# HGRN level products in blocks of 64 tokens, and another order for the end of the HGRN stage

## The reference, cut to what matters

```python
def step(s, inp):                       # one chunk, for HGRN
    qc, kc, vc, gc = inp
    g = jnp.cumsum(gc, axis=1)          # gc: log of the forget gate, per token and key channel
    o_inter = einsum('bthk,bhkv->bthv', qc * exp(g), s)
    diff = where(mask, g[:, :, None] - g[:, None, :], -inf)
    att = einsum('bthk,bshk,btshk->bhts', qc, kc, exp(diff))
    o_intra = einsum('bhts,bshv->bthv', att, vc)
    s_new = exp(g_last)[..., None] * s + einsum('bshk,bshv->bhkv', kc * exp(g_last - g), vc)
```

## Time and profile before

| | us |
|---|---|
| median of 3 runs | 1561.28 |
| lowest, highest | 1557.97, 1569.07 |
| the profiled execution | 1559.14 |
| its span, first to last instruction | 1557.1 |
| stage_hgrn in it | 534.9 to 575.1 |

### The profile page before, as it was taken

How to read it: one execution, slowest core, us unless ns; L and a number is a source line. 1 busy time by engine, 2 the same in 40 slices (tenths; PEclk the granted TensorE clock), 3 DMA queues, 4 the chain that set the end, 5 groups by cost and what they waited for, 6 DMA issues and landing times.

```text
span 1557.1 us, 37799 instructions
## 1 busy us (share of the span) xinstructions
PE 1522.2 (98%) x17035; PEld 971.1 (62%) x17035; DVE 527.0 (34%) x782; ACT 369.8 (24%) x560; POOL 44.9 (3%) x51
## 2 busy tenths in 40 slices
PE   9989999999999889999999999999999999999997
PEld 8976799999999866943533533534435435335344
DVE  6468656553569668451101111011011011010113
ACT  4248444442437467220000000000000000000001
POOL 0000000000000000000000000000000000000000
PEclk9999999999999999999999999999999999999999
DMA  9566645543445462699999999999999999999996
GB/s 356 202 230 211 198 128 167 184 162 143 136 167 176 154 159 64 239 367 420 369 388 418 417 410 417 410 417 415 411 416 418 411 417 417 412 417 415 412 413 234
DMA packets 144490, 479.48 MB, mean 308 GB/s; under 512 B 32184, under 2 KB 61632, under 8 KB 129747
## 3 DMA queue, kind: packets, MB, share of 16 engines
q1 hardware_dynamic: 141404, 469.07, 78.0%
q0 software_dynamic: 2064, 5.66, 0.9%
q10 hardware_dynamic: 871, 2.42, 0.4%
HBM read 463.55 MB, written 13.55 MB: 306 GB/s over the span
## 4 chain that ended last, share of the span: by engine, by line
PE 57%; DVE 0%; ACT 0%; DVEq 0%; issue 0%
PE ps L3146 37%; PE ps L3162 19%; PE ps L3122 0%; PE ps L3208 0%; PE ps L3190 0%; PE ps L3171 0%; PE ps L3196 0%; PE ps L3178 0%; DVE act L3367 0%; DVE act L3357 0%; DVE tail_rows L3357 0%; DVEq L3013 0%; ACT xn_tokens L3423 0%; DVE at_first L3244 0%; PE ps L3129 0%; ACT item_y L3408 0%
## 5 line engine op out<-in xcount | busy, mean ns | idle before, releaser
L3146 PE MATMUL ps<-up_ring,item_x 128*32 128x448 f32 x6000 | 565.6, 539 | 0.0
L3146 PEld LDWEIGHTS ps<-up_ring,item_x 128*32 128x32 f32 x6000 | 195.0, 110 | 365.5 <-issue 364.3
L3162 PE MATMUL ps<-down_ring,hid_t 128*32 128x256 f32 x5376 | 291.5, 379 | 0.0
L3162 PEld LDWEIGHTS ps<-down_ring,hid_t 128*32 128x32 f32 x5376 | 175.0, 110 | 117.6 <-issue 3.9
L3329 DVE TENSOR_TENSOR hid<-hid,ps 128x1344 f32<-128x1344 f32 x16 | 24.9, 1555 | 650.4 <-PE ps L3146 649.0
L476 DVE TENSOR_TENSOR w_lo_dense<-ring,w_hi_dense 128x2048 fp32r<-128x2048 f32 x53 | 121.3, 2291 | 99.5 <-ACT w_hi_dense L470 99.4
L470 ACT CAST w_hi_dense<-ring 128x2048 fp32r<-128x2048 f32 x53 | 100.9, 1903 | 89.4 <-PE ps L493 82.0
L3408 ACT COPY item_y<-ps 128x512 f32<-128x512 f32 x8 | 4.7, 586 | 422.2 <-PE ps L3162 422.2
L1684 PE MATMUL ps<-x_hi_dense,w_hi_dense 128*128 128x288 f32 x352 | 95.1, 296 | 1.8 <-PEq L1571 1.8
L1685 PE MATMUL ps<-x_lo_dense,w_hi_dense 128*128 128x288 f32 x352 | 94.9, 297 | 0.0
L3404 ACT ACTIVATE hid<-ps 128x1344 f32<-128x1344 f32 x16 | 20.6, 1290 | 265.6 <-PE ps L3146 243.2
(11 more groups left out here) (522 smaller groups left out, 1699.7 us busy)
## 6 DMA issues: line engine op xcount, KB each, us to landing
up_ring<-in_we_dram SPq DMA_DIRECT2D x250, 896.0 KB, 8.7
down_ring<-in_we_dram SPq DMA_DIRECT2D x112, 1024.0 KB, 11.2
ring<-in_w_ffn_dram SPq DMA_DIRECT2D x23, 1024.0 KB, 7.9
ring<-in_w_in_odd_dram SPq DMA_DIRECT2D x9, 2048.0 KB, 7.8
ring<-in_w_in_even_dram SPq DMA_DIRECT2D x5, 2048.0 KB, 16.3
ring<-in_w_ffn_dram SPq DMA_DIRECT2D x5, 2048.0 KB, 7.5
ring<-in_w_out_odd_dram SPq DMA_DIRECT2D x3, 2048.0 KB, 8.1
odd_layer<-in_we_dram SPq DMA_DIRECT2D x6, 896.0 KB, 12.2
```

The source lines that it names most:

```text
L3146: mm = pe.matmul(k.ps[32 * q:32 * q + 32, 3 * w + g, 0:FW], xg[:, c, g, :], block_of[:, q, :], start=c == 0, stop=c == DC - 1, skip_group_ ...
L3162: mm = pe.matmul(k.ps[32 * q:32 * q + 32, 6 + g // 2, 256 * (g % 2):256 * (g % 2) + 256], hidT[:, 2 * r + j, g, :], block_of[:, j, 256 * q ...
```

## The change

1. The diagonal and levels 0 to 4 are computed in blocks of 64x64 tokens: 16 products (32 pairs) where there were 32 (64 pairs). A gather is 512 columns wide where it was 256; the masks for it are made for blocks of 64.
2. The sample tokens get a place of their own: PSUM banks 7, 3 and 4 for the diagonal and levels 0 and 1, an own tile `att_samples`, own masks, and three small VectorE instructions of 32 columns.
3. ScalarE's copies into `att`: six (four of 32x32 for the samples, two of 64x512) where there were four, and ahead of level 5's copy, which now has to come after them. The constants' tables and `att_blocks` keep the same room in total.
4. The end: `state_samples` 0 to 3 stand together ahead of dot(7), in four banks (6, 7, 4, 2), so that `new_state` 0 to 3 follow one another; 4 and 5 come where 2 and 3 were, 6 and 7 where 4 and 5 were, ahead of the prompt's final state. `scale_state` comes earlier on ScalarE, and so do two copies of the convolution's last rows (`turn_last`, `take_last`).

```diff
@@ -106,14 +106,16 @@
-    s, q = p[:, None] % 32, np.arange(32)[None, :]
-    c["block_diagonal"] = (s == q) * 1.0
-    lv = []
-    for l in range(5):
-        h = 1 << l
-        lv.append((s // (2 * h) == q // (2 * h)) & (s % (2 * h) < h) & (q % (2 * h) >= h))
-    c["level"] = np.stack(lv, 1).reshape(P, -1)
-    c["room_for_gains"] = np.zeros((P, 672))
+    def block_masks(block, levels):
+        s, q = p[:, None] % block, np.arange(block)[None, :]
+        masks = [s == q]
+        for h in (1 << l for l in range(levels)):
+            masks.append((s // (2 * h) == q // (2 * h)) & (s % (2 * h) < h) & (q % (2 * h) >= h))
+        return np.stack(masks, 1).reshape(P, -1) * 1.0
+
+    c["level"] = block_masks(64, 5)
+    c["level_samples"] = block_masks(TS, 2)
+    c["room_for_gains"] = np.zeros((P, 384))
@@ -2043,7 +2045,8 @@
-        att32 = k.sb(s, "att_blocks", [P, 9, 32])
+        att64 = k.sb(s, "att_blocks", [P, 8, 64])
+        att_s = k.sb(s, "att_samples", [P, TS])
@@ -2082,14 +2085,15 @@
-        blocks_of = lambda bank: k.ps[:, bank, 0:9 * 32].rearrange("p (n j) -> p n j", j=32)
+        blocks_of = lambda bank: k.ps[:, bank, :].rearrange("p (n j) -> p n j", j=64)
...
+        samples_bank = lambda l: 3 + l
...
-        SIDE, SUM = (6, 7), (3, 5, 4)
+        SIDE, SUM = (6, 7, 4, 2, 6, 7, 6, 7), (3, 5, 4)
@@ -2150,23 +2154,24 @@
-                    mask = k.const("level")[:, 32 * l:32 * l + 32].bitcast(I32)
-                    n = 9 if l <= 1 else 8
-                    then(dve.copy_predicated(att32[:, 0:n, :], mask.unsqueeze(1).broadcast_to([P, n, 32]), blocks_of(bank_of(l))[:, 0:n, :]),
-                         n_["level_in"])
+                    mask = k.const("level")[:, 64 * l + 64:64 * l + 128].bitcast(I32)
+                    if l <= 1:
+                        dve.copy_predicated(att_s[:, :], k.const("level_samples")[:, TS * l + TS:TS * l + 2 * TS].bitcast(I32),
+                                            k.ps[:, samples_bank(l), 0:TS]).then_inc(*dve_step.up())
+                    then(dve.copy_predicated(att64[:, :, :], mask.unsqueeze(1).broadcast_to([P, 8, 64]), blocks_of(bank_of(l))), n_["level_in"])
...
-                    dve.wait_ge(*n_["state_dot"].at(i + 1 + (i >= 6)))
+                    dve.wait_ge(*n_["state_dot"].at(i + 1))
...
-                        dve.tensor_tensor(at, at, k.ps[:, SIDE[i % 2], :].rearrange("p (b v) -> p b v", b=4), ALU.add).then_inc(*n_["state_new"].up())
+                        dve.tensor_tensor(at, at, k.ps[:, SIDE[i], :].rearrange("p (b v) -> p b v", b=4), ALU.add).then_inc(*n_["state_new"].up())
...
-                                                       k.ps[:, SIDE[i % 2], P * (b % 4):P * (b % 4) + P], ALU.mult, ALU.add)
+                                                       k.ps[:, SIDE[i], P * (b % 4):P * (b % 4) + P], ALU.mult, ALU.add)
@@ -2179,8 +2184,10 @@
-                then(dve.tensor_tensor(att32[:, :, :], blocks_of(5), k.const("block_diagonal").unsqueeze(1).broadcast_to([P, 9, 32]), ALU.mult),
+                dve.tensor_tensor(att_s[:, :], k.ps[:, 7, 0:TS], k.const("level_samples")[:, 0:TS], ALU.mult).then_inc(*dve_step.up())
+                then(dve.tensor_tensor(att64[:, :, :], blocks_of(5), k.const("level")[:, 0:64].unsqueeze(1).broadcast_to([P, 8, 64]), ALU.mult),
...
+                dve.wait_ge(*dve_step.all())
@@ -2195,14 +2202,14 @@
                 new_state(3)
-                leave(0)
                 new_state(4)
                 new_state(5)
+                leave(0)
+                new_state(6)
                 leave(1)
...
                 dve.tensor_tensor(out[:, :, TP:T], by_head(k.ps[:, 2, 0:P]), rss, ALU.mult).then_inc(*n_["out"].up())
-                new_state(6)
                 new_state(7)
@@ -2264,27 +2271,30 @@
                 act.copy(kds[:, :], k.ps[:, 6, 0:P]).then_inc(*n_["kd_copied"].up())
+                take_last(1)
+                take_last(2)
+                act.wait_ge(*n_["zeroed"].at(2))
+                act.wait_ge(*n_["level_in"].at(6))
+                for a in range(0, P, TS):
+                    act.copy(att[a:a + TS, 8, a:a + TS], att_s[a:a + TS, :]).then_inc(*n_["blocks_in"].up())
+                for a in range(0, P, 64):
+                    act.copy(att[a:a + 64, 0:8, a:a + 64], att64[a:a + 64, :, :]).then_inc(*n_["blocks_in"].up())
+                act.wait_ge(*n_["blocks_in"].at(6))
                 act.wait_ge(*n_["inter_dot"].at(1))
                 act.copy(from_state[:, :], k.ps[:, 7, 0:P]).then_inc(*n_["inter_taken"].up())
-                act.wait_ge(*n_["zeroed"].at(2))
                 take_blocks(5)
-                take_last(1)
-                act.wait_ge(*n_["level_in"].at(6))
-                for a in range(0, P, 32):
-                    ins = act.copy(att[a:a + 32, :, a:a + 32], att32[a:a + 32, :, :])
-                ins.then_inc(*n_["blocks_in"].up())
+                scale_state(4)
                 take_blocks(6)
-                scale_state(4)
+                scale_state(5)
                 act.wait_ge(*dotted(7, 1))
                 act.copy(attx[:, :, :], k.ps[:, 3, :].rearrange("p (c n) -> p c n", c=4)).then_inc(*attx_in.up())
-                take_last(2)
                 act.wait_ge(*dt_turned.at(1))
...
                 square(0)
-                scale_state(5)
+                scale_state(6)
                 square(1)
@@ -2292,9 +2302,8 @@
-                scale_state(6)
...
-                act.wait_ge(*n_["state_dot"].at(7))
+                act.wait_ge(*n_["state_dot"].at(9))
@@ -2304,16 +2313,16 @@
-                        mm = pe.matmul(k.ps[TS * c:TS * c + TS, bank, 8 * 32:9 * 32], x1[:, c, TP:T], x2[:, c, TP:T], start=True, stop=True,
+                        mm = pe.matmul(k.ps[TS * c:TS * c + TS, bank, 0:TS], x1[:, c, TP:T], x2[:, c, TP:T], start=True, stop=True,
...
-                            for a in range(0, P, 32):
-                                at, n = slice(P * i + a, P * i + a + 32), 4 * i + c
-                                mm = pe.matmul(k.ps[a:a + 32, bank, 32 * n:32 * n + 32], x1[:, c, at], x2[:, c, at], start=True, stop=True,
+                            for a in range(0, P, 64):
+                                at, n = slice(P * i + a, P * i + a + 64), 4 * i + c
+                                mm = pe.matmul(k.ps[a:a + 64, bank, 64 * n:64 * n + 64], x1[:, c, at], x2[:, c, at], start=True, stop=True,
@@ -2334,17 +2343,19 @@
+                    if l == 5:
+                        pe.wait_ge(*n_["level_in"].at(3))
...
-                        pe.wait_ge(*n_["blocks_in"].at(1))
+                        pe.wait_ge(*n_["blocks_in"].at(7))
...
-                                mm = samples_dot(bank, x1, x2)
+                                mm = samples_dot(samples_bank(l), x1, x2)
@@ -2364,10 +2375,13 @@
                         pe.wait_ge(*n_["inter_taken"].at(1))
-                    if i >= 2:
-                        pe.wait_ge(*n_["state_new"].at(i - 1))
+                        pe.wait_ge(*last_copied.at(3))
+                    if i == 2:
+                        pe.wait_ge(*n_["blocks_in"].at(7))
+                    if i >= 4:
+                        pe.wait_ge(*n_["state_new"].at(i - 3 if i < 6 else i - 1))
                     r = slice(TS * c, TS * c + TS)
-                    pe.matmul(k.ps[:, SIDE[i % 2], :], kds[r, :], vbd[r, 4 * hf:4 * hf + 4, :], start=True, stop=True).then_inc(*n_["state_dot"].up())
+                    pe.matmul(k.ps[:, SIDE[i], :], kds[r, :], vbd[r, 4 * hf:4 * hf + 4, :], start=True, stop=True).then_inc(*n_["state_dot"].up())
 
@@ -2375,9 +2389,10 @@
-                samples_dot(5, k0, q).then_inc(*n_["diag_dot"].up())
+                samples_dot(7, k0, q).then_inc(*n_["diag_dot"].up())
...
+                pe.wait_ge(*n_["level_in"].at(1))
@@ -2387,7 +2402,10 @@
+                turn_last(1)
...
+                pe.wait_ge(*last_copied.at(1))
+                turn_last(2)
@@ -2396,14 +2414,10 @@
                 dot(5)
-                turn_last(1)
                 dot(6)
-                state_samples(0)
-                state_samples(1)
-                pe.wait_ge(*last_copied.at(1))
-                turn_last(2)
+                for i in range(4):
+                    state_samples(i)
                 dot(7)
-                pe.wait_ge(*last_copied.at(2))
                 for m, src in enumerate((dta["acum"], dt, dta["wend"])):
@@ -2427,32 +2441,30 @@
 
-                pe.wait_ge(*n_["blocks_in"].at(3))
+                pe.wait_ge(*n_["blocks_in"].at(8))
                 pe.wait_ge(*attx_in.at(1))
...
                 y_prompt(1)
-                state_samples(2)
-                state_samples(3)
+                state_samples(4)
+                state_samples(5)
                 pe.wait_ge(*dt_copied.at(5))
...
                 sum_squares(0)
-                pe.wait_ge(*last_copied.at(3))
+                pe.wait_ge(*n_["state_new"].at(4))
```

(8 more changed lines are left out.)

## The result

The changed kernel takes 1553.88 us (median of 20 runs, 1549.77 to 1564.95) against 1561.32 us (20 runs, 1557.33 to 1569.86). The ratio is 0.9958, 95% interval 0.9946 to 0.9971: 4.5 to 8.4 us faster, 6.6 by the ratio. The forecast was 4.6 us faster, 1556.0 us, in a range of 1551.5 to 1562.0. The profiled execution shows the stage from 535.95 to 568.65.

A forecast was written before the change was run, and what follows sets the result against it. A chain across engines with TensorE instruction halts bounds stage_hgrn, and a us saved there is one of the program; 4.4 - 0.9 + 1.1 = 4.6 us gives 1554.5 or 1556.7, 1556.0 us taken, range 1551.5 to 1562.0.

The forecast's parts named there:

- main term: Level products: with no halts for instruction pieces, dot(5) is done 4.4 us sooner.
- Matmul 175: End of an instruction piece in the stage, now in dot(3): needed at about 542.7, delivered by 542.3, no halt.
- The rival by which the halts stay: Level products: halts belong to the DMA load, not the count; vector work makes it 2.1 us slower; chance 0.08.
- the first rival: Product with the states: piece 303 comes late and halts it for 2 us; gain 2.6 us; chance 0.17.
- 64 pairs of 32 columns take about 1.2 us: Level products: TensorE's own time for one old set of pairs.
- I take 0.9: Level products: 32 pairs of 64x64 take 0.9 us a set, between 0.7 and about 2.
- The wide gather: VectorE's gather of 512 columns: 0.77 us, +0.33 over 256; +0.28 taken for each of six.
- the narrow steps: Three small VectorE instructions of 32 columns for the samples: 0.2 us each.
- Now the states are next to be late: Product with the states: its load lands 11.4 us after issue, 547.0 with 0.8 of issuing, a floor covering the vector work.
- The end's gain of 1.1: End of the stage: no state products behind the prompt's state; y_prompt to warming matmuls 10.9 us for 12.0.
- dot(7)'s delay: Four state products ahead of dot(7) take 2.26 us, putting it off by about 0.8; 0.9 in the sum.
- The clock at the product with the states: Rival: the product gets the upper clock, 1.8 us more, gain 6.4 us; chance 0.15. Forecast kept 3.58 us.

The follow-up runs named there:

- shift: Kernel before, plus 64 small matmul pairs at the end of TensorE's list of the stage ahead; stage 38.44 us.
- before_again: Kernel before, unchanged, traced a second time; stage 40.62 us.
- blocks_only: Kernel before with blocks of 64 and ScalarE's six copies, but the old order of the end; stage 33.58 us, ratio to before 0.9957.
- split2_shift: Changed kernel, states' product cut in two, ScalarE's sample copies behind the second square, 64 small pairs in the stage ahead; stage 31.81 us, ratio to before 0.9973.
- tail_only: Changed kernel with blocks of 32 again, keeping the new order of the end; stage 37.11 us, ratio to before 0.9995.
- onegroup: Changed kernel with all eight state products reading rows 0 to 31, so wrong sample states; stage 37.87 us.

## Why the prediction was right, and where its sizes were off

It was right in direction and range, and in the mechanism of its main term: the halts went. The stage's own gain was 7.5 us for 4.6, and what is missing lies in three terms, each too careful.

- The halts are deliveries of 256 instructions. Shown by `shift`, by `before_again` and by the packets of `q8 instruction`. That they would go was right as well, and for the reason given: a piece's end is reached later. Matmul 175 was forecast at 542.7, 7.8 us into the stage, and came 7.8 us in. (Matmul 47 was reached at 535.4 and not at 535.6, so the first delivery took 4.5 us.) The rival by which the halts stay fell; of the first rival (one comes late in the product with the states) 0.35 us came true.
- "64 pairs of 32 columns take about 1.2 us" was a misreading, without effect on the sum. The sets of 1.2 us ran at a granted clock of 0.50 (541.6 to 543.2 and 548.1 to 549.3 us); at 1.00 the pairs take 0.54. So "I take 0.9" for 32 pairs of 64x64 was thought of as a saving and is a doubling, 1.08 from start to start (1.15 to 1.33 with the last one's length), inside 0.7 to 2. The last half of a set was still hidden by the gathers.
- The wide gather costs 0.73 us (0.77 reckoned, then 0.72 taken), the narrow steps 0.1 of VectorE's time from start to start, not 0.2. With both, VectorE ran on without a wait for TensorE from 538.7 to 549.0.
- "Now the states are next to be late": the product started 11.5 us into the stage, for 12.1 forecast. In blocks_only it waited 0.43 us for the load itself, and again started 11.5 us in: the load is the floor. The time for issuing that was put on top of the 11.4 us (0.6 in the sum) should not have been added. +0.5 us.
- From y_prompt to the warming matmuls 10.9 us were forecast, 10.84 came. The end's gain of 1.1 less dot(7)'s delay was 0.2 in the forecast; `blocks_only` against the changed kernel shows 0.9, as the delay did not come: from the first state product to dot(7) it was 1.52 us before and is 1.07.
- 4.6 + 0.5 + 1.3 + 1.1 = 7.5 us.
- That a us of the stage is a us of the program: SSD kept its length, and 7.5 us lies in the interval of 4.5 to 8.4. The interval also holds 5 us, so this is borne out and not shown to the us; `split2_shift` does not fit it.
- The clock at the product with the states was the one large term left to a chance of 0.15. What sets it was not known then and is not now, so that 1.3 us of the gain came by luck.

The Trainium skill ("Runtime: NRT & Kernel Launch", Instruction fetch mechanics) has the block of 256, which these traces bear out at every halt (127 or 128 recorded pairs apart, packets of 16,384 bytes); that its cost is mostly hidden held after the change (0 to 0.4 us) and not before it (5.8 and 5.9 us).

## What to carry to other kernels

Count instructions, and not only their time, where many short ones follow one another beside large loads: if "issue" waits lie at a fixed distance in count, fewer and larger instructions can gain even where their own time grows. The packets of the instruction queue in the DMA rows show whether such a wait is a delivery. Before a duration is multiplied by a number, ask whether the instructions use the same part of the engine. When a wait goes, look at the next one in that place: here a load, ScalarE's list and the next piece of instructions each took over in turn.

## What was not expected of the hardware

Two executions of the same code had halts of 1.83, 2.08, 2.01 and of 0.84, 2.86, 2.10 us: single deliveries vary by 1 us, the sum by 0.1. One of 4.10 us was seen in `shift`; its packet started 5.0 us after the piece ahead of it was entered, at 540.57.

The granted clock fell to 0.50 in stretches in which TensorE worked, and not only behind idle time: in tail_only it was at 0.50 from 541.9 to 543.9 and at 1.00 for the product with the states at 552.3, and in onegroup it was at 0.50 from 564.6 on, behind 5.8 us in which TensorE was busy without a break. In the changed kernel TensorE never stood longer than 1 us in the stage, and the clock stayed at 1.00. What decides was not tried.
